# Two norms of a two-layer decoder trunk: sums with tokens on the partitions, the root on four columns, the result spread by products

## The chip, the cores and the metric

The kernel runs on one core of one Trainium2 chip, as one launch for the whole model of two layers. The metric is the device time of that launch in microseconds (us). TensorE (PE) multiplies, VectorE (DVE) and ScalarE (ACT) read its accumulation banks and work on SBUF, and GpSimd (POOL) does almost nothing after the start. SyncE (SP) issues the loads of weights.

## The reference, cut to what matters

x has 512 tokens of 1024 channels. Each of the two layers computes three token mixers in parallel, a cross-attention on 256 memory tokens and a SwiGLU feed-forward part. Two of its norms are touched here:

```
def gmlp(uv_in, ln_g, ln_b, w_s, b_s):
    u, v = split(gelu(uv_in), 2)
    mu  = mean(v, axis=-1)
    var = mean((v - mu)**2, axis=-1)
    v   = (v - mu) * rsqrt(var + EPS) * ln_g + ln_b        # 512 channels
    ...                                                    # mixing within chunks of 128 tokens
    return u * mixed

def mla(c_q, ...):
    q = (rms_norm(c_q, q_norm) @ w_uq)                     # c_q has 384 channels
    ...
rms_norm(x, g) = x * rsqrt(mean(x*x) + EPS) * g
```

So for every token a sum over channels is needed, then root and reciprocal, then that number is applied to every channel of the token.

## The kernel before, in words

All activations lie transposed: channels on the 128 partitions, the 512 tokens along the free axis, so a tile is 128 x 512 in fp32. A weight matrix is cut in units of 128 output columns. For a unit SP loads `raw` (three slots), ScalarE rounds it to `wH` (`split`, L964), VectorE makes the rest `wL` (`weight_low`, L1370), and TensorE makes three products for each 128 input channels, `wH` with `hH`, `wH` with `hL`, `wL` with `hH` (L577 to L579), with 512 columns each. A unit with 1024 input channels has 24 products.

`PLAN` is a list of steps that every engine walks. TensorE walks it as it stands. VectorE and ScalarE walk `READERS_PLAN`, the same list with four norm steps moved a little ahead. Each engine does for a step only what is its own, strictly in order, with a wait on a counter wherever it needs another engine's result. TensorE's results go to seven banks in rotation (`take`): each taking waits for the reader of the bank's previous content. `LEFT_OUT` and `known["pad"]` keep the slots and the rotation the same for both passes of the layer loop.

A sum over channels is a sum over partitions. The usual way in this kernel: VectorE and ScalarE add up the squares of the tiles into one tile of 128 x 512, TensorE multiplies it by a 128 x 128 matrix of ones, `ones`, as one fp32 product of 512 columns, so that every partition of the bank holds the sum of every token. ScalarE takes the root of the 128 x 512 bank into a tile, and VectorE its reciprocal.

**The gated unit (gMLP).** `v` is `gv`, four tiles, `u` is `gu`, four tiles. `gm_mean` (L697) is the sum for the mean. VectorE subtracts it (L1470), ScalarE squares (L1106), VectorE adds into `gsum` (L1475). `gm_var`, after the unit `gu` 2, is the product of ones (L697), the root on ScalarE into `rstd` (L1110), the reciprocal on VectorE (L1479), four products of `gv` with `rstd` (L1482) and four scalings (L1485). `gm_vt` later transposes `gv` on TensorE (L703), ScalarE copies it to `gvt` (L1114), and `gm_mix` (L711) mixes the tokens. Between them stand the forget gate of the recurrent mixer (`f_2` on ScalarE: L1092 to L1098; `f_3` on VectorE: `hk`, `hlf`, L1513, L1518), pieces of the rotary angles (`angle`, VectorE L1346 to L1363), the units `gu` 3, `hi`, `hq` and `hg`, and `sin`, in which VectorE makes `segM` (L1457) that the first `hg_exp` product reads (L738).

**The queries' norm.** `norm_q`, after the unit `ckv` 0, is the product of ones with `sqs` (L799), the root into `rstd` (L1182), the reciprocal (L1594). The evictions of the query heads (`mq`, L1333) multiply by `rstd`.

**The key-value norm** is done in the other way already. `norm_kv` (L805) makes four products in which the 128 tokens of a block of `ytmp` are the stationary side and one column of `ones` streams, so that tokens land on partitions and the bank has four columns. Root (L1185) and reciprocal (L1597) work on 128 x 4. `rkv` (L811) spreads a column along the tokens by four products of the column, broadcast to 128 x 128, with the identity `ident`, and ScalarE copies the bank to the tile `rkv` (L1190).

`mst` is four columns of the tile `columns`. An fp32 product appears in the trace as two records.

Of the kernel before, what the change touches and what calls it, by code (L numbers as in the profile page):

```python
# [24 lines left out]
ACT = mybir.ActivationFunctionType  # L25
AX = mybir.AxisListType

P = 128
DM, T, L, NM = 1024, 512, 2, 256
EPS = 1e-6  # L30
KT = DM // P
TT = T // P
QR, KVR, NOPE, ROPE, VD, HA = 384, 256, 64, 32, 64, 8
HG, CH = 4, 64
# [70 lines left out]
def plan():  # L105

    u = lambda name, j=0: ("u", name, j)
    p = [("lb",), u("gv", 0), u("gv", 1), ("norm", "mix"), u("gv", 2), u("gv", 3), ("angle", 0), u("hf", 0), ("gm_sum",), ("gm_ws",)]
    p += [u("gu", 0), ("gm_mean",), u("gu", 1), ("f_1", 0), u("gu", 2), ("gm_var",), ("f_2", 0), ("angle", 1), u("gu", 3), ("f_3", 0), ("angle", 2)]
# [12 lines left out]
    p += [("cq_split",), u("ckv", 0), ("norm_q",), u("ckv", 1), u("kr"), ("kr_swap",), u("q", 0), ("norm_kv",), ("hg_norm", HG - 1)]  # L122
# [81 lines left out]
def build(nc, a, out, known):  # L204
# [7 lines left out]
    with ExitStack() as ctx:  # L212
# [10 lines left out]
        def did(engine, *step):  # L223

            count[engine] = count.get(engine, 0) + 1
            counted["mark"][step] = (engine, phase[0], count[engine])
            return sem(engine + "_done"), 1

        def after(l, *step):

            engine, of, n = mark.get(step, ("tensor", "before", 1))
            s = sem(engine + "_done")
            if of == "before":
                return s, n
            b, t = base.get(engine, 1), total.get(engine, 1)
            if of == "after":
                return s, b + L * t + n
            if phase[0] == "after":
                return s, b + (L - 1) * t + n
            return s, l * t + (b + n)  # L240
# [168 lines left out]
        def bank(*step):  # L409
            return PS[:, bank_of.get(step, 0), :]  # L410
# [106 lines left out]
        def _(pe):  # L517
# [4 lines left out]
            def take(l, step, reader, keep=False):  # L522


                b = 7 if keep else turn[0] % 7
                turn[0] += not keep
                if fresh[b]:

                    pe.wait_ge(*before(l, *last_reader.get(b, ("x0", 0))))
                elif readers[b]:  # L530
                    pe.wait_ge(*after(l, *readers[b]))
                fresh[b] = False
                readers[b] = reader
                counted["bank"][step] = b
                return PS[:, b, :]
# [135 lines left out]
            with pe.Fori(0, L) as l:  # L671
# [3 lines left out]
                for step in PLAN:  # L675
# [18 lines left out]
                    elif kind in ("gm_mean", "gm_var"):  # L694
                        o = take(l, (kind,), ("gm_c", 3) if kind == "gm_mean" else ("gm_std",))
                        pe.wait_ge(*after(l, kind + "_sum"))
                        nc.tensor.matmul(o, ones[:], gsum[:], start=True, stop=True).then_inc(*did("tensor", kind))  # L697
                    elif kind == "gm_vt":
# [97 lines left out]
                    elif kind == "norm_q":  # L796
                        o = take(l, (kind,), (kind + "_std",))
                        pe.wait_ge(*after(l, kind + "_sum"))
                        nc.tensor.matmul(o, ones[:], sqs[:], start=True, stop=True).then_inc(*did("tensor", kind))  # L799
# [125 lines left out]
        def _(act):  # L925
# [51 lines left out]
            with act.Fori(0, L) as l:  # L977
# [16 lines left out]
                for step in READERS_PLAN:  # L994
# [113 lines left out]
                    elif kind == "gm_var":  # L1108
                        act.wait_ge(*after(l, "gm_var"))
                        nc.scalar.activation(rstd[:], bank("gm_var"), ACT.Sqrt, scale=1.0 / 512, bias=EPS).then_inc(*did("scalar", "gm_std"))  # L1110
# [68 lines left out]
                    elif kind == "norm_q":  # L1179
                        act.wait_ge(*after(l, kind))  # L1180
                        act.wait_ge(*after(l, "o_n", HG - 2))
                        nc.scalar.activation(rstd[:], bank(kind), ACT.Sqrt, scale=1.0 / QR, bias=EPS).then_inc(*did("scalar", kind + "_std"))  # L1182
# [101 lines left out]
        def _(dve):  # L1284
# [87 lines left out]
            with dve.Fori(0, L) as l:  # L1372
# [12 lines left out]
                for step in READERS_PLAN:  # L1385
# [91 lines left out]
                    elif kind == "gm_var":  # L1477
                        dve.wait_ge(*after(l, "gm_std"))
                        V.reciprocal(rstd[:], rstd[:]).then_inc(*did("vector", "gm_rstd"))  # L1479
                        dve.wait_ge(*own(l, "vector"))  # L1480
# [111 lines left out]
                    elif kind == "norm_q":  # L1592
                        dve.wait_ge(*after(l, "norm_q_std"))
                        V.reciprocal(rstd[:], rstd[:]).then_inc(*did("vector", "norm_q_r"))  # L1594
# [84 lines left out]
                    elif kind == "u":  # L1679
# [51 lines left out]
                        elif name == "q":  # L1731
                            dve.wait_ge(*after(l, *step))
                            dve.wait_ge(*own(l, "vector"))
# [91 lines left out]
```

## Time and profile before

| | |
|---|---|
| median of 3 runs | 2244.11 us (2242.25 to 2244.37) |
| the profiled execution, its own time | 2240.72 us |
| its span, first to last instruction | 2238.9 us |
| granted TensorE clock, mean | 0.995 |
| busy: PE, DVE, ACT, POOL | 2195.5 us, 1341.1 us, 995.3 us, 9.2 us |
| HBM traffic over the span | 87 GB/s |

The page tells for each engine how long it was busy, and follows the chain of work that ended last back from the end. The timeline lists instructions of one engine in order of time, with the start, the duration, and in brackets the idle time of the engine before it and what ended it. Neighbouring instructions of the same kind are merged with a count (x4). PEld is the loading of TensorE's stationary side, which overlaps the products.

### The profile page before, as it was taken

How to read it: one execution, taken by the hardware profiler on the slowest of the kernel's cores; microseconds unless marked ns; L12 is line 12 of the kernel's file. 1: busy time of each engine (PE TensorE's matmuls, PEld its weight loads, DVE VectorE, ACT ScalarE, POOL GpSimd, SP SyncE). 2: the span in 40 equal slices, each digit the busy share in tenths (PEclk: the TensorE clock that was granted, in tenths of full speed). 3: DMA queues.
4: the chain of work that ended last, by engine and by line, in shares of the span. 5: the costliest groups of instructions: out<-in, count | busy, mean ns of one | idle time of the engine just before them, and what ended most of it. 6: DMA issues, size and time to landing. Idle time of an engine off the chain costs nothing.

```text
span 2238.9 us, 31689 instructions
## 1 busy us (share of the span) xinstructions
PE 2195.5 (98%) x10441; PEld 1785.5 (80%) x10441; DVE 1341.1 (60%) x2099; ACT 995.3 (44%) x1451; POOL 9.2 (0%) x12
## 2 busy tenths in 40 slices
PE   7999999999999999999999999999999999999998
PEld 6877787778888888888877877777788888888887
DVE  7867777666565544443378677776666655444432
ACT  5665545454443433322255555454444443233223
POOL 1000000000000000000000000000000000000000
PEclk9999999999999999999999999999999999999999
DMA  6222222224343233333252222122343333333331
GB/s 177 64 76 57 67 59 58 61 73 120 106 122 95 83 111 99 95 90 102 83 136 59 67 66 71 43 56 68 101 116 100 114 94 94 95 103 95 97 95 64
DMA packets 368238, 197.55 MB, mean 88 GB/s; under 512 B 24284, under 2 KB 361544, under 8 KB 368072
## 3 DMA queue, kind: packets, MB, share of 16 engines
q1 hardware_dynamic: 362584, 185.81, 29.8%
q10 hardware_dynamic: 5488, 9.64, 1.4%
q8 instruction: 90, 1.47, 0.3%
q14 instruction: 76, 0.62, 0.1%
HBM read 192.14 MB, written 2.10 MB: 87 GB/s over the span
## 4 chain that ended last, share of the span: by engine, by line
PE 85%; DVE 7%; issue 4%; ACT 3%; DMA 0%; DVEq 0%; ACTq 0%; SPq 0%
PE PS L577 24%; PE PS L579 24%; PE PS L578 24%; PE PS L823 2%; PE PS L846 2%; PE PS L758 1%; DVE attn L1556 1%; DVE rstd L1576 1%; DVE mprod L1552 1%; DVE dec L1538 1%; PE PS L833 1%; PE PS L652 1%; PE PS L654 1%; PE PS L653 1%; ACT wH L964 1%
## 5 line engine op out<-in xcount | busy, mean ns | idle before, releaser
L964 ACT ACTIVATE wH<-raw 128x1024 fp32r<-128x1024 f32 (+4 forms) x406 | 384.1, 947 | 943.9 <-PE PS L579 908.6
L577 PE MATMUL PS<-hH,wH 128*128 128x512 f32 (+1 forms) x1680 | 666.8, 397 | 4.8 <-DVE gate L1333 3.4
L579 PE MATMUL PS<-hH,wL 128*128 128x512 f32 (+1 forms) x1680 | 656.0, 390 | 0.0
L578 PE MATMUL PS<-hL,wH 128*128 128x512 f32 (+1 forms) x1680 | 655.7, 390 | 0.0
L1370 DVE TENSOR_TENSOR wL<-raw,wH 128x1024 fp32r<-128x1024 f32 (+4 forms) x406 | 437.4, 1078 | 177.8 <-ACT wH L964 177.1
L577 PEld LDWEIGHTS PS<-hH,wH 128*128 128x128 f32 (+1 forms) x1680 | 316.1, 188 | 76.6 <-DVE gate L1333 4.3
L578 PEld LDWEIGHTS PS<-hL,wH 128*128 128x128 f32 (+1 forms) x1680 | 316.2, 188 | 67.1 <-issue 2.9
L579 PEld LDWEIGHTS PS<-hH,wL 128*128 128x128 f32 (+1 forms) x1680 | 315.8, 188 | 67.4
L1333 DVE TENSOR_TENSOR gate<-PS,rh 128x512 f32<-128x512 f32 x92 | 63.6, 691 | 154.6 <-PE PS L579 154.0
L579 PE MATMUL PS<-fH,wL 128*128 128x512 f32 x352 | 136.9, 389 | 0.0
L577 PE MATMUL PS<-fH,wH 128*128 128x512 f32 x352 | 136.9, 389 | 0.0
L578 PE MATMUL PS<-fL,wH 128*128 128x512 f32 x352 | 136.9, 389 | 0.0
L1316 DVE TENSOR_TENSOR xT<-xT,PS 128x512 f32<-128x512 f32 x48 | 33.0, 688 | 132.4 <-PE PS L579 132.4
L1333 DVE TENSOR_TENSOR fm<-PS,rh 128x512 f32<-128x512 f32 x44 | 30.4, 691 | 131.2 <-PE PS L579 131.2
L578 PEld LDWEIGHTS PS<-fL,wH 128*128 128x128 f32 x352 | 66.1, 188 | 13.8
L577 PEld LDWEIGHTS PS<-fH,wH 128*128 128x128 f32 x352 | 66.1, 188 | 13.7
L579 PEld LDWEIGHTS PS<-fH,wL 128*128 128x128 f32 x352 | 66.1, 188 | 13.6
L1556 DVE TENSOR_REDUCE attn<-mprod 128x128 f32<-128x896 f32 x32 | 56.2, 1756 | 1.1
L577 PE MATMUL PS<-mgH,wH 128*128 128x512 f32 x128 | 49.8, 389 | 0.0
L578 PE MATMUL PS<-mgL,wH 128*128 128x512 f32 x128 | 49.8, 389 | 0.0
L579 PE MATMUL PS<-mgH,wL 128*128 128x512 f32 x128 | 49.8, 389 | 0.0
L577 PE MATMUL PS<-xoH,wH 128*128 128x512 f32 x128 | 49.8, 389 | 0.0
(354 smaller groups left out, 3256.0 us busy)
## 6 DMA issues: line engine op xcount, KB each, us to landing
raw<-in_w_in SPq DMA_DIRECT2D x106, 512.0 KB, 3.9
raw<-in_ffn_w_in SPq DMA_DIRECT2D x88, 512.0 KB, 3.8
raw<-in_xa_w_kv SPq DMA_DIRECT2D x32, 512.0 KB, 3.8
raw<-in_ffn_w_out SPq DMA_DIRECT2D x32, 512.0 KB, 3.9
raw<-in_w_mix_out SPq DMA_DIRECT2D x16, 512.0 KB, 4.1
raw<-in_xa_w_q SPq DMA_DIRECT2D x16, 512.0 KB, 4.2
raw<-in_xa_w_o SPq DMA_DIRECT2D x16, 512.0 KB, 3.9
raw<-in_ffn_w_out SPq DMA_DIRECT2D x16, 384.0 KB, 3.3
```

The source lines that it names most:

```text
L577: nc.tensor.matmul(o, w0, xh(k0 + k), start=(first and k == 0), stop=False)
L578: nc.tensor.matmul(o, w0, xl(k0 + k), start=False, stop=False)
L579: ins = nc.tensor.matmul(o, w1, xh(k0 + k), start=False, stop=(last and k == kts - 1))
L652: nc.tensor.matmul(xv_banks[i], xh, w0, start=(kk_ == 0), stop=False)
L653: nc.tensor.matmul(xv_banks[i], xh, w1, start=False, stop=False)
L823: nc.tensor.matmul(o[:, 0:n], mq[0:96, h % 2, i * P:n], mk[0:96, h % 2, 0:n], start=True, stop=False)
L846: ins = nc.tensor.matmul(oa_bank[r, kb * P:T], mv[:, kb, h * VD:(h + 1) * VD], mpt[:, PT_OFF[kb]:PT_OFF[kb] + n], start=(kb == 0), stop=(k ...
L964: nc.scalar.activation(wH[:, PLACE[n] % NS, 0:w], raw[:, PLACE[n] % NR, 0:w], ACT.Copy).then_inc(*did("scalar", "hi", n))
L1316: V.tensor_tensor(xT[:, j, :], xT[:, j, :], bank(*step) if name != "fo" else bank("fo", j), ALU.add)\
L1333: V.tensor_tensor(dst, src, scale, ALU.mult).then_inc(*did("vector", *me))
L1370: V.tensor_tensor(wL[:, s, 0:w], raw[:, r, 0:w], wH[:, s, 0:w].bitcast(F32), ALU.subtract).then_inc(sem("weights_low"), 1)
L1556: V.tensor_reduce(attn[:, i, :], mprod[:].rearrange("p n t -> p t n"), AX.X, ALU.add)\
```

## The change

The variance of the gated unit and the queries' norm are computed as the key-value norm is. Four products with one streaming column each take the place of the product with `ones`. Root and reciprocal work on `mst`, 128 x 4. Two new steps spread the result: `gm_rs`, after the unit `gu` 3, and `rq`, after the unit `ckv` 1. In each, TensorE makes four products of a broadcast column with `ident`, and ScalarE copies the bank to `rstd`. The eight operations of VectorE on `gv` move from the step `gm_var` to `gm_rs`. The eviction of the first query head waits for `rq`.

```diff
-    p += [u("gu", 0), ("gm_mean",), u("gu", 1), ("f_1", 0), u("gu", 2), ("gm_var",), ("f_2", 0), ("angle", 1), u("gu", 3), ("f_3", 0), ("angle", 2)]
+    p += [u("gu", 0), ("gm_mean",), u("gu", 1), ("f_1", 0), u("gu", 2), ("gm_var",), ("f_2", 0), ("angle", 1), u("gu", 3), ("gm_rs",), ("f_3", 0), ("angle", 2)]
...
-    p += [("cq_split",), u("ckv", 0), ("norm_q",), u("ckv", 1), u("kr"), ("kr_swap",), u("q", 0), ("norm_kv",), ("hg_norm", HG - 1)]
+    p += [("cq_split",), u("ckv", 0), ("norm_q",), u("ckv", 1), ("rq",), u("kr"), ("kr_swap",), u("q", 0), ("norm_kv",), ("hg_norm", HG - 1)]
...
+                    elif kind == "gm_var":
+                        o = take(l, (kind,), ("gm_std",))
+                        pe.wait_ge(*after(l, kind + "_sum"))
+                        for i in range(TT):
+                            ins = nc.tensor.matmul(o[:, i:i + 1], gsum[:, i * P:(i + 1) * P], ones[:, 0:1], start=True, stop=True)
+                        ins.then_inc(*did("tensor", kind))
+                    elif kind in ("gm_rs", "rq"):
+                        o = take(l, (kind,), (kind,))
+                        pe.wait_ge(*after(l, "gm_rstd" if kind == "gm_rs" else "norm_q_r"))
+                        for i in range(TT):
+                            ins = nc.tensor.matmul(o[:, i * P:(i + 1) * P], mst[:, i:i + 1].broadcast_to([P, P]), ident[:], start=True, stop=True)
+                        ins.then_inc(*did("tensor", kind + "_b"))
...
-                        nc.tensor.matmul(o, ones[:], sqs[:], start=True, stop=True).then_inc(*did("tensor", kind))
+                        for i in range(TT):
+                            ins = nc.tensor.matmul(o[:, i:i + 1], sqs[:, i * P:(i + 1) * P], ones[:, 0:1], start=True, stop=True)
+                        ins.then_inc(*did("tensor", kind))
...
-                        nc.scalar.activation(rstd[:], bank("gm_var"), ACT.Sqrt, scale=1.0 / 512, bias=EPS).then_inc(*did("scalar", "gm_std"))
+                        nc.scalar.activation(mst, bank("gm_var")[:, 0:TT], ACT.Sqrt, scale=1.0 / 512, bias=EPS).then_inc(*did("scalar", "gm_std"))
+                    elif kind in ("gm_rs", "rq"):
+                        act.wait_ge(*after(l, kind + "_b"))
+                        if kind == "rq":
+                            act.wait_ge(*after(l, "o_n", HG - 2))
+                        nc.scalar.activation(rstd[:], bank(kind), ACT.Copy).then_inc(*did("scalar", kind))
...
-                        act.wait_ge(*after(l, "o_n", HG - 2))
-                        nc.scalar.activation(rstd[:], bank(kind), ACT.Sqrt, scale=1.0 / QR, bias=EPS).then_inc(*did("scalar", kind + "_std"))
+                        nc.scalar.activation(mst, bank(kind)[:, 0:TT], ACT.Sqrt, scale=1.0 / QR, bias=EPS).then_inc(*did("scalar", kind + "_std"))
...
-                        V.reciprocal(rstd[:], rstd[:]).then_inc(*did("vector", "gm_rstd"))
-                        dve.wait_ge(*own(l, "vector"))
+                        V.reciprocal(mst, mst).then_inc(*did("vector", "gm_rstd"))
+                    elif kind == "gm_rs":
+                        dve.wait_ge(*after(l, "gm_rs"))
...
-                        V.reciprocal(rstd[:], rstd[:]).then_inc(*did("vector", "norm_q_r"))
+                        V.reciprocal(mst, mst).then_inc(*did("vector", "norm_q_r"))
...
+                            if j == 0:
+                                dve.wait_ge(*after(l, "rq"))
```

**VectorE in the gated unit**, the order of its instructions before, from the low part of a weight at the end of `gu` 2 on (`turns` belongs to the angles; a REGISTER_ALU row sets up a wait; line numbers are each kernel's own):

```order
L1370 TENSOR_TENSOR wL<-raw,wH 128x1024
L1478 REGISTER_ALU
L1479 RECIPROCAL rstd<-rstd 128x512
L1480 REGISTER_ALU
L1482 TENSOR_TENSOR gv<-gv,rstd 128x512 x4
L1483 REGISTER_ALU
L1485 TENSOR_SCALAR gv<-gv,cur 128x512 x4
L1452 REGISTER_ALU
L1357 TENSOR_SCALAR turns<-turns 32x512
```

and with the change, from the last angle operations of that step on:

```order
L1470 REGISTER_ALU
L1377 SCALAR_TENSOR_TENSOR red_148<-turns,red_148 32x512
L1470 REGISTER_ALU
L1377 SCALAR_TENSOR_TENSOR red_148<-turns,red_148 32x512
L1702 REGISTER_ALU
L1351 TENSOR_TENSOR gu<-PS,rh 128x512
L1387 REGISTER_ALU
L1388 TENSOR_TENSOR wL<-raw,wH 128x1024
L1499 REGISTER_ALU
L1501 TENSOR_TENSOR gv<-gv,rstd 128x512 x4
L1502 REGISTER_ALU
L1504 TENSOR_SCALAR gv<-gv,cur 128x512 x4
```

The eight operations on `gv` stood before the angle step and the eviction of `gu` 3. They now stand behind both and behind the low part of the next weight, with a wait of their own ahead of them (L1499).

**ScalarE in the same place**, before, from the high part of a weight at the start of `gu` 3 on:

```order
L957 REGISTER_ALU
L961 REGISTER_ALU
L964 ACTIVATE wH<-raw 128x1024
L1004 REGISTER_ALU
L1006 ACT_TABLE_LOAD
L1006 ACTIVATE gu<-gu 128x512
L957 REGISTER_ALU
L961 REGISTER_ALU
L964 ACTIVATE wH<-raw 128x1024
```

and with the change:

```order
L971 REGISTER_ALU
L975 REGISTER_ALU
L978 ACTIVATE wH<-raw 128x1024
L1018 REGISTER_ALU
L1020 ACT_TABLE_LOAD
L1020 ACTIVATE gu<-gu 128x512
L1126 REGISTER_ALU
L1129 ACTIVATE rstd<-PS 128x512
L971 REGISTER_ALU
L975 REGISTER_ALU
L978 ACTIVATE wH<-raw 128x1024
```

The copy of the spread root (L1129) stands right behind the activation of `gu` 3 and ahead of the next weight.

## Rows read from the trace of the kernel before

**Rows 1.** The page: busy time of the engines, and the chain by engine.
```profile
PE 2195.5 (98%) x10441; PEld 1785.5 (80%) x10441; DVE 1341.1 (60%) x2099; ACT 995.3 (44%) x1451; POOL 9.2 (0%) x12
...
PE 85%; DVE 7%; issue 4%; ACT 3%; DMA 0%; DVEq 0%; ACTq 0%; SPq 0%
```

**Rows 2.** TensorE's waits: who for whom, us in total, times, longest.
```profile
PE PS L738 <- DVE segM L1457: 2.1, 2, 1.0
```

**Rows 3.** Timeline, TensorE at `gm_var`: start us, us, engine, line, operation [idle before].
```profile
68.62 0.39 PE L579 MATMUL PS<-hH,wL 128*128 128x512 f32 x1
68.85 1.02 PE L697 MATMUL PS<-gsum,ones 128*128 128x512 f32 x2
...
69.94 0.40 PE L578 MATMUL PS<-hL,wH 128*128 128x512 f32 x1
```

**Rows 4.** Timeline, TensorE at `norm_kv` and the head norm behind it.
```profile
348.39 0.40 PE L579 MATMUL PS<-cqH,wL 128*96 128x512 f32 x1
348.63 0.95 PE L805 MATMUL PS<-ones,ytmp 128*128 128x1 f32 x8
349.44 1.10 PE L795 MATMUL PS<-onrm,ones 128*128 128x512 f32 x2
...
350.62 0.39 PE L578 MATMUL PS<-ckL,wH 128*64 128x512 f32 x1
```

**Rows 5.** Timeline, TensorE at `rkv`.
```profile
351.30 0.40 PE L578 MATMUL PS<-ckL,wH 128*64 128x512 f32 x1
351.53 0.40 PE L579 MATMUL PS<-ckH,wL 128*64 128x512 f32 x1
351.77 1.05 PE L811 MATMUL PS<-ident,columns 128*128 128x128 f32 x8
...
352.89 0.39 PE L632 MATMUL PS<-wL,ckH 128*128 128x512 f32 x1
```

**Rows 6.** The tile `columns`: duration ns min/median/max, first and last start.
```profile
L1185 ACT ACTIVATE columns<-PS x2: 173/174/174, 349.6 to 1452.7; 128x4 f32<-128x4 f32 x2
L1597 DVE RECIPROCAL columns<-columns x2: 165/166/166, 350.0 to 1453.0; 128x4 f32<-128x4 f32 x2
```

**Rows 7.** Timeline, VectorE at the unit `kr`, after the queries' norm.
```profile
346.83 0.69 DVE L1333 TENSOR_TENSOR krt<-PS,rh 96x512 f32<-96x512 f32 x1 [0.50 <-PE PS L579]
```

**Rows 8.** Timeline, VectorE from `gm_var` to `segM`, first layer.
```profile
72.57 3.35 DVE L1479 RECIPROCAL rstd<-rstd 128x512 f32<-128x512 f32 x1 [1.21 <-ACT rstd L1110]
75.96 2.50 DVE L1482 TENSOR_TENSOR gv<-gv,rstd 128x512 f32<-128x512 f32 x4
...
80.44 0.42 DVE L1357 TENSOR_SCALAR turns<-turns 32x512 f32<-32x512 f32 x1
...
84.78 0.48 DVE L1513 TENSOR_SCALAR hk<-hk,lbc 128x512 f32<-128x512 f32 x1
...
96.50 1.23 DVE L1370 TENSOR_TENSOR wL<-raw,wH 128x1024 fp32r<-128x1024 f32 x1 [1.36 <-ACT wH L964]
...
98.24 0.68 DVE L1457 CAST segM<-seg 128x1024 fp32r<-128x1024 f32 x1
```

**Rows 9.** Timeline, ScalarE from `gm_var` to `hq`, first layer.
```profile
71.94 0.60 ACT L1110 ACTIVATE rstd<-PS 128x512 f32<-128x512 f32 x1
...
78.67 1.28 ACT L1006 ACT_TABLE_LOAD   x1
83.77 0.63 ACT L1006 ACTIVATE gu<-gu 128x512 f32<-128x512 f32 x1 [3.81 <-DVE gu L1333]
84.31 1.05 ACT L964 ACTIVATE wH<-raw 128x1024 fp32r<-128x1024 f32 x1
...
92.94 0.63 ACT L1010 ACTIVATE hq<-hq 128x512 f32<-128x512 f32 x1 [4.73 <-DVE hq L1333]
```

**Rows 10.** Timeline, TensorE at the transposes of `gv` and at `segM`.
```profile
86.08 1.91 PE L703 MATMUL PS<-ident,gv 128*128 128x128 f32 x16
...
99.05 0.49 PE L738 MATMUL PS<-segM,lfH 128*128 128x512 f32 x1 [1.04 <-DVE segM L1457]
```

More of the change, by code:

```diff
@@ L693, in _ @@
                         ins.then_inc(*did("tensor", "gm_ws"))
-                    elif kind in ("gm_mean", "gm_var"):
-                        o = take(l, (kind,), ("gm_c", 3) if kind == "gm_mean" else ("gm_std",))
+                    elif kind == "gm_mean":
+                        o = take(l, (kind,), ("gm_c", 3))
                         pe.wait_ge(*after(l, kind + "_sum"))
                         nc.tensor.matmul(o, ones[:], gsum[:], start=True, stop=True).then_inc(*did("tensor", kind))
+                    elif kind == "gm_var":
[10 more added lines that the diff above has]
+                        ins.then_inc(*did("tensor", kind + "_b"))
                     elif kind == "gm_vt":
```

## The prediction

> **What bounds the kernel now.** I read the page's busy shares and its chain first [rows 1]: TensorE is busy for 98% of the span and carries 85% of the chain that ended last, VectorE 7%, ScalarE 3%. So a microsecond added to TensorE's own stream counts in full, and a microsecond taken from VectorE counts only where TensorE waits for VectorE. I then asked for TensorE's waits. In the two stretches that the change touches one wait stands: the product on `segM` waits for VectorE, 2.1 us in the two layers together [rows 2]. After the queries' norm no wait of TensorE hangs on it. Last I read the timelines of both stretches, engine by engine, to price the operations and to follow VectorE's queue to that wait. In the gated unit's stretch VectorE is far behind TensorE: ScalarE waits 3.81 us for the eviction of the last `gu` and starts on it at 83.77 [rows 9], while TensorE, with 22 steps of 0.23 us after 69.94 [rows 3], was through with it by 75.4.
>
> **TensorE, what goes.** At each place one fp32 product of 512 columns is removed. [rows 3] show it between two ordinary products: L579 starts at 68.62, the next L578 at 69.94. An ordinary step is 0.23 us (351.30 to 351.53 in [rows 5]), and two would have taken 0.46, so the product costs 1.32 - 0.46 = 0.86 us.
>
> **TensorE, what comes.** The kernel already does both new kinds of product for the key-value norm. Sums by columns: in [rows 4] L579 starts at 348.39 and the second ordinary product after the group at 350.62, 2.23 us later. Off go 0.46 for two steps and 0.86 for the 512-column product L795 in between: 0.91 us for four sums (eight records). The spread: in [rows 5] L579 starts at 351.53 and L632 at 352.89, 1.36 us; less 0.46 it is 0.90 us for four products of 128 columns. Both are priced by the very same forms in the same kind of neighbourhood, so I take these values. The bounds are nothing at all, if they hid beside their neighbours, and the whole 0.95 and 1.05 us that the two groups span in [rows 4, 5], if nothing overlapped: 0.19 more or 1.81 less a place than these values. **Net 0.91 + 0.90 - 0.86 = 0.95 us a place**, four places (two in each of two layers): 3.8 us of TensorE time, if every one of them reaches the end.
>
> The Trainium skill's page "TensorE: Matmul & The Clock Gate" (Back-to-back issue gap) gives a warm product of 1 to 64 columns some 25 ns and one of 128 columns 56 ns, start to start, when it is isolated from weight loads. By that, eight and eight records would make 0.65 us where the trace has 1.81, and the net would be -0.21 us a place. The trace disagrees, since here each of these products brings its own weights [rows 4, 5]; I go by the rows.
>
> **VectorE and ScalarE at the queries' norm.** The 3.35 us reciprocal becomes one on four columns, 0.17 us [rows 6], the root 0.17 instead of 0.60, and a copy of 0.60 comes in. It is worth nothing: a few VectorE operations later VectorE sits idle 0.50 us until TensorE has finished `krt` [rows 7], so it had already caught up, and from there on everything follows TensorE. The first reader of the spread norm, the eviction of `q` head 0, comes only after `krt` in VectorE's order, and ScalarE's copy stands two units ahead of it. So both layers pay the full 0.95: **+1.9 us**.
>
> **VectorE and ScalarE in the gated unit.** Here the order matters. Before, VectorE runs [rows 8]: reciprocal at 72.57, four products with `rstd` from 75.96, four scalings up to 80.44, angle, last `gu` eviction, low part of a weight, then `hk` at 84.78. From the reciprocal to `hq` the timeline gives it no idle time, and the wait of [rows 2] is the end of that queue: `hq` late, so ScalarE's `Silu` waits 4.73 us for it [rows 9], behind it the four `gvt` copies and a weight's high part, then VectorE's low part (idle 1.36 for it), `lfL`, `segM` at 98.24, and TensorE starts at 99.05 after 1.04 us of idleness [rows 8, 10].
>
> The change takes 3.35 - 0.17 + 0.43 = 3.6 us off VectorE's start of this queue. But it moves the eight operations on `gv` behind the last `gu` step, and makes them wait for ScalarE's copy of the spread root, which stands behind ScalarE's exponentials, one weight, the table load for `Gelu` and `Gelu` itself. That queue has no wait in it: it only shifts by the shorter root. The load of [rows 9] at 78.67 comes at 78.67 - 0.43 = 78.24 and lasts 1.28; `Gelu` starts at 79.52 (its `gu`, which TensorE finishes at 75.4, is evicted well before), the copy at 80.06 (0.54 later, as the weight follows `Gelu` in [rows 9]), and it ends 0.60 later at 80.66. VectorE starts the products with `rstd` at 80.69 and needs 80.44 - 75.96 = 4.48 us for the eight: `hk` starts at 85.17 instead of 84.78. **VectorE's queue is 0.39 us later, not 3.6 earlier**: it now idles first for the weight's high part, then for the copy. Behind the waiting products on VectorE are `hk`, `hlf`, the angle and `hq`; all of them move by 0.39, and `segM` with them. TensorE arrives 0.95 later, at 98.96 instead of 98.01, and starts at 99.05 + 0.39 = 99.44. So of its 0.95 only 0.39 remains, the rest goes into the stall, which shrinks from 1.04 to 0.5 us. The transposes of `gv`, 86.08 before and 87.03 now [rows 10], find the whole of `gv` finished at 85.2, with 1.9 us to spare. Two layers: **+0.8 us**. ScalarE's extra copy needs no table load of its own, since a weight is copied right behind `Gelu`, at 84.31, without one [rows 9].
>
> Other edits cost nothing: each layer takes two more accumulation banks, in rotation, but every bank that comes up earlier was read out long before (the nearest readers belong to the unit before last or earlier), and the padding that squares the rotation at the layer's end falls among the output units, where TensorE waits for nothing. No DMA is added.
>
> **Sum.** 1.9 + 0.8 = +2.7 us. Against the profiled execution, 2240.72 us, that is 2243.4; the median of the three runs is 2244.11, so I say **2246.8 us**. About 0.2%, 4.5 us, is what a measurement of this kernel can tell from no change, so this is within it.
>
> **Rivals.**
> 1. VectorE's relief does arrive (the copy is earlier than I reckon, or the queue is not tied to it). For: 3.6 us are really taken off. Then TensorE finds `segM` ready but for 1.04 - 0.95 = 0.09 us, and each layer gains 0.09 there: 1.9 - 0.2 = +1.7, 2245.8 us. Against: ScalarE's queue of [rows 9] has no slack to give.
> 2. Slower by over 0.2%: the hand-over through ScalarE is the new bound. If the copy of the spread root costs one more table load (1.28, as each in [rows 9]), or waits that long for anything, VectorE's queue and `segM` are 0.39 + 1.28 = 1.67 us late in each layer, and TensorE with them: 1.9 + 3.3 = +5.2, 2249.3 us. It decides from 1.3 us of lateness a layer (4.5 = 1.9 + 2 x 1.3), a copy 0.9 us later than reckoned. For: the copy is the last in a row of seven operations and two table loads, and VectorE is strictly in order. Against: [rows 9], and the compiled order has no load between `Gelu` and the copy.
> 3. The small products hide beside their neighbours and cost next to nothing. Then the queries' norm gains 0.86 in each layer, the gated unit stays on VectorE's 0.39: -1.7 + 0.8 = -0.9, 2243.2 us. [rows 4, 5] speak against it. This is the side to which the page named above leans.
> 4. The change doesn't do what it says, in time: TensorE pays 0.95 everywhere and VectorE's queue plays no part, because the stall is not the queue's end. +3.8, 2247.9 us.
>
> **Chances.** The forecast, with rival 4 as its near neighbour, 0.70; rival 1 0.12; rival 3 0.03; rival 2 0.11; the rest, mostly a measurement that is off by more than the runs show, 0.04. All but rival 2 and part of the rest lie within 4.5 us: same 0.84, slower 0.12, faster 0.04. Even the lower bounds of every part together, -0.86 twice and -0.09 twice, give -1.9 us, so faster needs a disturbance. The range goes from 2243.0 (rival 3) to 2250.0 (rival 2 and 0.7 for the scatter of the runs).
>
> **What would show it.** In the profile after: each sum group and each spread group at some 0.9 us of TensorE; VectorE idle before the products of `gv` with `rstd`, ended by ScalarE's copy; `hk` 0.4 us later than before; the wait on `segM` down to about 0.5 us a layer, all in both layers; `krt` still waiting for TensorE. Wrong would be: the wait on `segM` grown or gone, a wait of TensorE before the transposes of `gv`, a table load beside the new copy, or a span that moves by more than 4.5 us.

## The result

| | kernel before | changed kernel |
|---|---|---|
| median, fastest and slowest of 20 runs each on one chip | 2242.15 us (2238.51 to 2245.55) | 2246.11 us (2243.35 to 2249.52) |
| span of the profiled execution | 2238.9 us | 2242.8 us |
| granted TensorE clock, mean | 0.995 | 0.995 |

The ratio is 1.0018, 95% interval 1.0011 to 1.0025: 4.0 us slower (2.5 to 5.6). The prediction was +2.7 us and 2246.8 us. The kernel before ran here 2 us below the median shown ahead of the prediction, so it is the difference that is to be compared, not the closeness of the two totals. The changed kernel's 20 runs had a mean granted clock of 0.9940; for the 20 runs of the kernel before beside them the clock is not on record, and in 62 later runs it was 0.9946. So up to about 1 us of the 4.0 may be clock.

The page of the changed kernel answers to [rows 1]:

```profile
PE 2199.1 (98%) x10497; PEld 1791.5 (80%) x10497; DVE 1328.9 (59%) x2099; ACT 996.3 (44%) x1455; POOL 9.1 (0%) x12
...
PE 80%; DVE 9%; issue 5%; ACT 4%; DMA 1%; ACTq 0%; DVEq 0%; SPq 0%
```

VectorE has 12.2 us less to do, TensorE 3.6 us more, close to the 3.9 us by which the span grew. The chain is now followed further along VectorE, but that is one way back among several that end together; it says nothing of where the 4 us come from. The waits of TensorE (who for whom, us in total, times, longest) say more:

```profile
PE PS L750 <- DVE segM L1475: 1.2, 2, 0.8
...
PE PS L837 <- DVE mq L1631: 0.6, 1, 0.6
```

The wait of [rows 2] went from 2.1 to 1.2 us (0.45 in the first layer, 0.80 in the second), and there is one that the kernel before does not have: the first scores of the latent attention wait for VectorE's rotated queries, `mq`.

TensorE at `gm_var` and at the first spread, first layer (start us, us, engine, line, operation):

```profile
68.42 0.39 PE L579 MATMUL PS<-hH,wL 128*128 128x512 f32 x1
68.65 0.95 PE L702 MATMUL PS<-ones,gsum 128*128 128x1 f32 x8
...
69.78 0.40 PE L578 MATMUL PS<-hL,wH 128*128 128x512 f32 x1
...
74.81 0.39 PE L579 MATMUL PS<-hH,wL 128*128 128x512 f32 x1
75.04 1.05 PE L708 MATMUL PS<-ident,columns 128*128 128x128 f32 x8
...
76.17 0.39 PE L578 MATMUL PS<-hL,wH 128*128 128x512 f32 x1
```

These answer to [rows 3 to 5]. The sums take 69.78 - 68.42 - 0.46 = 0.90 us, the spread 76.17 - 74.81 - 0.46 = 0.90 us. Predicted were 0.91 and 0.90.

VectorE from the reciprocal on, beside [rows 8], with the idle time before an operation and what ended it in brackets:

```profile
71.94 0.18 DVE L1497 RECIPROCAL columns<-columns 128x4 f32<-128x4 f32 x1 [0.78 <-ACT columns L1124]
...
78.06 1.23 DVE L1388 TENSOR_TENSOR wL<-raw,wH 128x1024 fp32r<-128x1024 f32 x1 [2.13 <-ACT wH L978]
80.49 2.50 DVE L1501 TENSOR_TENSOR gv<-gv,rstd 128x512 f32<-128x512 f32 x4 [1.20 <-ACT rstd L1129]
...
84.86 0.48 DVE L1532 TENSOR_SCALAR hk<-hk,lbc 128x512 f32<-128x512 f32 x1
...
98.33 0.68 DVE L1475 CAST segM<-seg 128x1024 fp32r<-128x1024 f32 x1
```

And ScalarE ahead of them, beside [rows 9]:

```profile
78.04 1.28 ACT L1020 ACT_TABLE_LOAD   x1
79.34 0.63 ACT L1020 ACTIVATE gu<-gu 128x512 f32<-128x512 f32 x1
79.88 0.58 ACT L1129 ACTIVATE rstd<-PS 128x512 f32<-128x512 f32 x1
```

VectorE saved 3.2 us on the reciprocal and stood idle for 2.13 + 1.20 of them, first for a weight's high part and then for the copy of the spread root. `hk` starts at 84.86, where it was 84.78. No table load came with the copy. TensorE at `segM`, beside [rows 10]:

```profile
94.96 3.74 PE L723 MATMUL PS<-gwT,gvt 128*128 128x128 f32 x32
99.14 0.49 PE L750 MATMUL PS<-segM,lfH 128*128 128x512 f32 x1 [0.45 <-DVE segM L1475]
...
1203.03 0.49 PE L750 MATMUL PS<-segM,lfH 128*128 128x512 f32 x1 [0.80 <-DVE segM L1475]
```

The second layer is not a copy of the first. There ScalarE's table load ahead of the root starts 1.76 us later than before (1174.34 against 1172.58) while TensorE is 1.43 us later, so 0.33 us of lateness was in the queue before the change acted, and it comes out at `segM`: 0.80 instead of 0.45.

**Where the 3.9 us of the span lie.** The unit products can be paired one by one between the two kernels. The start of one, changed kernel less kernel before, is a curve that moves only where something differs. It starts at -0.24 us (-0.20 ahead of the gated unit's sums) and ends at +3.82:

| place | shift of TensorE | 1st layer | 2nd layer |
|---|---|---|---|
| gated unit, from the sums to the spread group | up | +0.98 | +0.97 |
| wait for `segM` smaller | down | -0.69 | -0.35 |
| queries' norm | up | +0.91 | +0.91 |
| first scores, `mq` late | up | 0 | +0.50 |
| between the layers, a DMA issue of ScalarE (below) | up | +0.45 | |
| half clock at other places (below) | both | | -1.26 + 1.60 |

The rest, +-0.1 us at a time, is drift. The first three lines, the ones that the prediction priced, make +2.7 us; the other three make +1.3.

### The profile page after: what moved, and what is told of

It reads as the page before. It is cut to its first block, busy times and chain, and to the rows that moved or that the text cites. A ratio compares the mean times of both kernels' runs of the same rounds, so it can differ in the third digit from the quotient of the medians.

```text
span 2242.8 us, 31821 instructions
## 1 busy us (share of the span) xinstructions
PE 2199.1 (98%) x10497; PEld 1791.5 (80%) x10497; DVE 1328.9 (59%) x2099; ACT 996.3 (44%) x1455; POOL 9.1 (0%) x12
## 4 chain that ended last, share of the span: by engine, by line
PE 80%; DVE 9%; issue 5%; ACT 4%; DMA 1%; ACTq 0%; DVEq 0%; SPq 0%
PE PS L577 23%; PE PS L578 23%; PE PS L579 23%; PE PS L860 2%; PE PS L837 2%; PE PS L770 1%; DVE attn L1575 1%; DVE mprod L1571 1%; DVE rstd L1595 1%; DVE dec L1557 1%; PE PS L847 1%; ACT wH L978 1%; PE PS L654 1%; PE PS L652 1%; PE PS L653 1%
## 5 line engine op out<-in xcount | busy, mean ns | idle before, releaser
L579 PE MATMUL PS<-hH,wL 128*128 128x512 f32 (+1 forms) x1680 | 655.2, 390 | 0.0
L579 PEld LDWEIGHTS PS<-hH,wL 128*128 128x128 f32 (+1 forms) x1680 | 315.5, 188 | 67.1
L579 PE MATMUL PS<-fH,wL 128*128 128x512 f32 x352 | 136.9, 389 | 0.0
L579 PEld LDWEIGHTS PS<-fH,wL 128*128 128x128 f32 x352 | 66.1, 188 | 13.7
L579 PE MATMUL PS<-mgH,wL 128*128 128x512 f32 x128 | 49.8, 389 | 0.0
```

What stands on the lines that cost most here:

```text
L579: ins = nc.tensor.matmul(o, w1, xh(k0 + k), start=False, stop=(last and k == kts - 1))
```

## The experiments

Ten further runs were made: nine other kernels, and the changed one once more. Differences of 1 us are at the edge of what such runs tell, so each verdict rests on the ratio with its interval and on the shift curve of the trace. A third number, called "at equal clock" below, comes from a line put through the 161 runs whose clock is on record, without those of the last two kernels (time against the run's mean granted clock, one level for each kernel; for the kernel before these are the 62 runs of the later rounds): 1.83 us less for each 0.001 of clock, with a scatter of 0.96 us that is left. By it the changed kernel is 3.0 us (+-0.5) slower than the one before. It is an adjustment worked out after the runs, not a measurement of its own, and it is fair only if a kernel doesn't itself change how often the clock falls, which was not tried.

### Each half alone

`e1_gated_only` keeps the gated unit's half of the change and puts the queries' norm back, `e2_queries_only` the reverse.

```
 e1   norm_q:  matmul(o, ones[:], sqs[:]) ; Sqrt -> rstd ; reciprocal(rstd)        # as before
      PLAN:    ... u("ckv", 1), u("kr") ...                                        # no ("rq",)
 e2   gm_var:  matmul(o, ones[:], gsum[:]) ; Sqrt -> rstd ; reciprocal(rstd), gv * rstd
      PLAN:    ... u("gu", 3), ("f_3", 0) ...                                      # no ("gm_rs",)
```

> The gated unit's part of the change alone; the queries' norm is as before. Theory (TensorE's own price, less what the wait on segM swallows): each layer pays 0.9 us of TensorE, and the wait on segM shrinks from 1.04 to about 0.5 us, so 0.3 to 0.4 us a layer remain, +0.6 to +0.8 us against the kernel before. Rival (TensorE pays everything): +1.9 us, and the wait on segM stays at 1.04. In the trace: TensorE is +0.9 later behind the spread in the first layer and +0.3 to +0.4 later from segM on, against the kernel before, and krt and the first scores show no further step.

> The queries' norm alone in the new way; the gated unit is as before. Theory: 0.95 us of TensorE in each layer, all of it in the end, +1.9 us against the kernel before; VectorE's 3.2 us a layer are worth nothing. Rival (VectorE's relief is worth something behind it, at the rotary chain and the first scores): between 0 and +1. In the trace: one step of +0.9 to +1.0 us of TensorE in each layer, between the units ckv 0 and kr, and no step in the gated unit.

Measured: `e1_gated_only` 1.0002 of the time before (0.9993 to 1.0011), at equal clock +0.6 us (+-0.6); `e2_queries_only` 1.0004 (0.9995 to 1.0014), at equal clock +1.8 us (+-0.6). Neither half can be told from no change by the ratio alone. The traces are sharper. In the gated half the shift goes from -0.88 to +0.11 at the spread and to -0.59 at `segM`: +0.29 net, with the wait at 0.44 and 0.46 us in the two layers. In the queries' half it goes from -0.49 to +0.43 and stays, +0.92 and +0.91 in the two layers, and `segM` keeps its 1.04 us. Two halves make 0.6 + 1.8 = 2.4, the whole 3.0: additive within the errors. Neither half's trace has a wait for `mq` at the first scores, so 0.5 us of what is left may be that wait.

### The changed kernel once more

> The changed kernel once more, for a second profile of the same program. The theory is that only two steps of the first comparison belong to the change: one spread group a place, +0.90 us each, less what comes back at segM. Those steps must stand again: TensorE idle 0.45 before the first product with segM in both layers, and the spread groups at 0.90. The rival is that everything between the two profiles belongs to the change: the 1.1 us by which ScalarE's DMA issue of seg was longer at the layer boundary, the 0.5 us at the first scores, and the two stretches at half clock (1233.4 to 1236.5 and 1318.7 to 1321.9). By the first theory these three stand elsewhere or are gone in this profile; by the rival they stand at the same places with the same sizes.

One run, 2244.03 us, span 2242.3. The places of the change stand at +0.91 to +0.97 us, the wait for `segM` at 0.47 and 0.60. Of the other steps, **one does not repeat and two do**. The layer boundary costs nothing here, with ScalarE's issue of `seg` at 1.38 us (it was 1.99 in the first profile, and 0.52 to 1.95 in kernels with nothing of the change). The two stretches at half clock stand where they were and as long: the granted clock is 0.88 from 1226 to 1240 us and 0.88 from 1311 to 1325 in both profiles. They are not the change's for all that: `e4_segm_early` and `e9_angle_alone`, which hold nothing of it, have 0.88 and 0.88 too, and it is the profile of the kernel before that differs, with 0.76 and 1.00. (Another stretch, at 213 us in the first profile, stands at 130 us in this one.) And the late `mq` is here again, in both layers:

```profile
PE PS L837 <- DVE mq L1631: 1.4, 2, 0.8
```

So the theory was wrong on the first scores, which belong to the change after all, and the rival on the boundary; the repeated half clock, which the rival had right, comes from something that the kernels have in common.

### The wait at the first scores

Before the scores two DMAs on ScalarE's queue swap the halves of the queries. ScalarE's queue in the changed kernel, first and second layer:

```profile
359.12 1.16 ACTq L1192 DMA_DIRECT2D spare<-mq  x2
...
1464.54 1.67 ACTq L1192 DMA_DIRECT2D spare<-mq  x2
```

The second issue is 0.5 us longer; the key-value norm's copy, `mk` and the rotation stand behind it, and TensorE waits. Instructions themselves come by DMA, on a queue of their own (page of the changed kernel):

```profile
q8 instruction: 90, 1.47, 0.3%
```

Ninety packets, one in 25 us. Their moment, read in half microseconds, against the issue:

| kernel, layer | packet on q8 | issue, its length | from TensorE's last L579 before the scores to the next L579 |
|---|---|---|---|
| before, both | none near | 358.15 and 1461.22, 1.16 | 3.58 and 3.61 |
| changed, 1st | 360.0 to 360.5 | 359.12, 1.16 | 3.59 |
| changed, 2nd | 1464.5 to 1465.0 | 1464.54, **1.67** | 4.12 |
| changed again, 1st | 359.0 to 359.5 | 358.66, **1.64** | 4.09 |
| changed again, 2nd | 1464.0 to 1464.5 | 1463.73, **1.88** | 4.33 |
| queries alone, 2nd | 1469 | 1461.15, 1.16 | |

(None near: none from 345 us to the first layer's scores, and none within 10 us of the second issue.) Four rows are few, but there are eight such pairs of issues in a layer, and with 12 traces 192 of them. In 180 no packet of q8 was under way during the pair, and it took 1.15 to 1.17 us every time. In the other 12 one was: ten of these took longer, 1.21 to 2.33 us, and the two that did not had their packet start in the last 0.3 us. The kernel before has one too (2.30 us at 369.64, and TensorE doesn't wait there). A kernel with products added ahead should move the packet off the issue. That is one of the two last kernels, and both also double a suspected cost:

```
 e10  norm_q:       for i in range(TT)   ->  for i in list(range(TT)) * 2      # the four sums twice
 e11  gm_rs, rq:    for i in range(TT)   ->  for i in list(range(TT)) * 2      # the four spreads twice
```

> The changed kernel with the four one-column sums of the queries' norm issued twice (same result). Two things are read. First the price of such a group in TensorE's stream: 0.90 us more at the queries' norm of each layer than the changed kernel shows there (+0.95 against the kernel before, so +1.85 in this one). Second the wait of TensorE for mq at the first scores. Theory: it is there because a transfer of instructions (queue q8, one every 25 us or so) lies at the same moment as ScalarE's DMA issue for the swap of the queries' halves, at 359 to 361 and at 1464 us in the changed kernel, and at 366 us or later in the queries' part alone; the issue then takes 1.6 to 1.9 us instead of 1.16. Four more products before it bring that transfer some 4 us earlier, away from the issue: the issue is back at 1.16 us, TensorE's wait for mq is gone in the first layer, and the whole is +0.9 x 2 - 0.5 to -1.2. Rival: the longer issue comes with the kernel's two new steps together, by whatever cause but not by that transfer's place, and stands here again at 1.6 us or more with the wait of 0.6 to 0.8 us.

Measured: the shift against the changed kernel rises from 3.70 to 4.59 (first layer) and from 7.41 to 8.30 (second) at the norm, 0.89 us for one more group. The sums twice, on TensorE's timeline:

```profile
338.16 0.39 PE L579 MATMUL PS<-hH,wL 128*128 128x512 f32 x1
338.39 1.84 PE L812 MATMUL PS<-ones,sqs 128*128 128x1 f32 x16
...
340.42 0.40 PE L578 MATMUL PS<-hL,wH 128*128 128x512 f32 x1
```

340.42 - 338.16 - 0.46 = 1.80 us for two groups. And the other half of the question:

```profile
363.71 1.16 ACTq L1192 DMA_DIRECT2D spare<-mq  x2
...
1472.84 1.16 ACTq L1192 DMA_DIRECT2D spare<-mq  x2
```

The packets start at 362.35 and 1471.40 us, ahead of the issues, moved by 2.3 and 1.8 us against them and not by the 4 expected; both issues are short, the wait for `mq` is gone, and the stretch at the scores takes 3.60 and 3.59 us again. In the changed kernel's first profile the first layer was short already, so this takes the wait away where it had been in three layers of four. The total is not to be read (one run, 2252.57 us at a clock of 0.992: some 3 us each were lost at half clock at 277 and at 1387 us, where the changed kernel's profile has no such stretch).

> The changed kernel with the four spread products issued twice in both places, in the gated unit and in the queries' norm. Theory: each doubled group costs TensorE 0.90 us once more at its place. In the gated unit the copy of the root is that much later for ScalarE and VectorE, but the values stood ready there with under 1 us to spare, so the wait at segM grows or stays: +0.9 at the spread, and of that 0.4 or less comes back at segM. At the queries' norm +0.9 more stays to the end. In all +2.5 to +3.6 us against the changed kernel. The transfer of instructions on q8 lies 8 products, some 8 us, earlier than in the changed kernel, and the issue for the queries' swap is at 1.16 us. Rival: the second group hides behind the weight loads of the first and adds less than half of 0.90.

One run, 2245.04 us, span 2243.3: **only +0.5 us on the span** of the changed kernel, where +2.5 to +3.6 had been expected. The price of a doubled group was right, +0.89 to +0.91 at each of the four places. What was wrong was the part given back. At `segM` all of it came back, 0.91 us in the first layer and 1.04 in the second, at the layer boundary 0.42, and at the second layer's scores another 0.51, since the packets start at 357.15 and 1462.64 us, ahead of the issues at 359.93 and 1465.54 (3.7 and 3.3 us earlier against them, where 8 had been expected), and both issues take 1.16. TensorE's timeline before `segM`'s product:

```profile
95.80 3.74 PE L723 MATMUL PS<-gwT,gvt 128*128 128x128 f32 x32
99.29 0.47 PE L750 MATMUL PS<-segM,lfH 128*128 128x512 f32 x1
```

So at the wait for `segM` the changed kernel still had 0.9 us to give, although its row says 0.45. The queue of VectorE did not move (`hk` at 84.82 us against 84.86), as the prediction's reading has it: the copy of the root waits for `Gelu` on ScalarE, not for TensorE.

### What a row of idle time is worth

`e3_rs_ahead` is the changed kernel in which ScalarE copies the spread root ahead of its work on `gu` 3, and VectorE multiplies by it ahead of its own. `e4_segm_early` is the kernel before, with the cast of `segM` in step `gm_ws`, long before it is needed.

```
 e3   READERS_PLAN: (("norm", "ffn"), 2), (("rkv",), 1), + (("gm_rs",), 1)
 e4   step "sin":   - V.tensor_copy(segM[:], seg[:])
      step "gm_ws": + V.tensor_copy(segM[:], seg[:])
```

> The changed kernel with one edit: ScalarE and VectorE take the step gm_rs ahead of gu 3 (one entry in the list of moved steps). Theory (VectorE's queue is set by ScalarE's copy, which stands behind a weight, a table load and Gelu): the copy comes at about 77.0 instead of 79.9 us, the products with rstd at 77.6 instead of 80.5, hk 1.1 us earlier (the eviction of gu 3 and a weight's low part now stand ahead of it), the wait on segM disappears in both layers, and TensorE gains what is left of it, 0.45 and up to 0.8 us: -0.9 to -1.2 us against the changed kernel, so +1.5 to +3 against the kernel before. Rival (the wait on segM has another cause): the copy comes earlier and the wait stays.

> The kernel before, with one edit: VectorE makes segM in the step gm_ws, 44 us earlier, instead of at the end of its queue. Theory (the wait on segM is the end of VectorE's queue): TensorE then waits for lfL, 0.6 us earlier, so -0.6 us a layer, -1.2 us in all against the kernel before. Rival (the wait belongs to segM itself, its load or its making): the wait goes entirely, -1.0 us a layer, -2.1 us.

Measured: `e3_rs_ahead` 1.0004 of the time before (0.9995 to 1.0013), at equal clock 2.6 us below the changed kernel; more than expected. `e4_segm_early` 0.9989 (0.9980 to 0.9998). Their timelines at `segM` explain the first:

```profile
94.82 3.74 PE L723 MATMUL PS<-gwT,gvt 128*128 128x128 f32 x32
98.31 0.47 PE L750 MATMUL PS<-segM,lfH 128*128 128x512 f32 x1
```

That is `e3_rs_ahead`. First below is the mix in the kernel before, whose product on `segM` is at 99.05 [rows 10], then `e4_segm_early`, where the wait is now for VectorE's `lfL`:

```profile
94.20 3.81 PE L711 MATMUL PS<-gwT,gvt 128*128 128x128 f32 x32
...
93.82 3.81 PE L711 MATMUL PS<-gwT,gvt 128*128 128x128 f32 x32
98.16 0.49 PE L738 MATMUL PS<-segM,lfH 128*128 128x512 f32 x1 [0.53 <-DVE lfL L1338]
```

From the first product of the mix to the first with `segM`, first layer:

| kernel | idle in the row | from mix to `segM` | more than without a wait |
|---|---|---|---|
| before | 1.04 | 4.85 us | 1.36 |
| with the early cast | 0.53 | 4.34 | 0.85 |
| changed | 0.45 | 4.18 | 0.69 |
| `e3_rs_ahead`, and the doubled spread | none | 3.49 | 0 |

**A stop cost some 0.3 us more here than its idle row says** (0.24 to 0.32): the row of idle time begins when the last product is through, while in the unbroken stream of `e3_rs_ahead` the product on `segM` starts at 98.31, 0.25 us before the row of the mix ends (94.82 + 3.74). The ends of such rows are modelled, so the distances between starts are what counts. Behind the eight products on `segM` the kernel before loses another 0.26 us: 0.39 and 0.33 us to the next two unit products instead of 0.23 each in `e3_rs_ahead`. In all it lost 1.6 us a layer here, not 1.04. The expectations below reckon with 1.5.

With that known, three versions were made to take the loss away.

```
 e7   the gated unit's half of the change + e3's entry + e4's early cast
 e8   the kernel before + e4's early cast + READERS_PLAN: (("angle", 1), 2)
 e9   the kernel before                    + READERS_PLAN: (("angle", 1), 2)
```

The entry for `angle` lets VectorE do the angles' second step (2.5 us) ahead of the reciprocal, in the 1.21 us in which it waits for ScalarE's root [rows 8].

> The gated unit's part of the change alone (the queries' norm as in the kernel before), with VectorE's multiplies by the spread root taken ahead of its reading of gu 3, and segM made from seg back in step gm_ws. A stop of TensorE has cost more in the runs so far than its idle row says: from the first product of the mix to the first product with segM TensorE took 4.85 us with a row of 1.04, 4.18 with 0.45 and 3.49 with none, so a row of 1.04 hides a loss of 1.36, and another 0.15 lies behind the products with segM. Theory: this kernel pays +0.90 a layer for the spread group and gets the whole 1.5 back, so -0.6 a layer, -1.2 us in all, 0.9995 of the time before, with no idle row before segM's product and the span from mix to segM at 3.49. Rival: the early cast of segM takes 0.7 us of VectorE at a place where something else waits, and the gain is half or none: 1.0000.

> The kernel before, nothing of the change in it: segM made from seg back in step gm_ws, and VectorE takes the angles' second step (four operations, 2.5 us) ahead of the reciprocal for the gated unit, into the 1.2 us that it stood idle there. Theory: the stall before segM's products was VectorE's queue and nothing else, and both edits together remove 0.7 and 1.2 us of that queue, more than the 1.36 us that the stall cost; TensorE goes from the mix to the products with segM in 3.49 us instead of 4.85 and starts behind them without the gap of 0.15, -1.5 us a layer, -3.0 us in all, 0.9987 of the time before. Rival: the angles' step is longer than the idle time it fills, the reciprocal and with it the multiplies for the gated unit's values come 1.3 us later, and TensorE waits for them at the transposes (1.3 us a layer) instead: 1.0000 to 1.0012.

> The kernel before with the angles' second step alone taken ahead of the reciprocal by VectorE; segM is made where it was. Theory: VectorE reaches segM 1.2 us earlier, the idle row of 1.04 before segM's product shrinks to 0 to 0.2 us, and the kernel gains 0.9 to 1.2 us a layer, some -2.1 us, 0.9991. Rival as for both together: the reciprocal is late for the transposes and TensorE waits there, 1.0000 to 1.0012.

| kernel | ratio to before, 95% | shift at `segM`, layer 1, layer 2 | at equal clock |
|---|---|---|---|
| `e7_gated_ahead_segm` | 0.9988 (0.9978 to 0.9997) | -0.71, -0.72 | -3.3 (+-0.6) |
| `e8_seg_and_angle` | 0.9985 (0.9976 to 0.9994) | -1.68, -1.70 | -4.5 (+-0.6) |
| `e9_angle_alone` | 0.9996 (0.9987 to 1.0005) | -1.28, -1.30 | -3.2 (+-0.6) |

In `e8_seg_and_angle` the loss is gone, with nothing of the change in it. TensorE:

```profile
93.89 3.74 PE L711 MATMUL PS<-gwT,gvt 128*128 128x128 f32 x32
97.38 0.47 PE L738 MATMUL PS<-segM,lfH 128*128 128x512 f32 x1
```

VectorE, whose idle time of 1.21 before the reciprocal is filled:

```profile
71.12 0.42 DVE L1357 TENSOR_SCALAR turns<-turns 32x512 f32<-32x512 f32 x1
71.58 0.68 DVE L1359 SCALAR_TENSOR_TENSOR red<-turns,ang 32x512 f32<-32x512 f32 x1
72.29 1.40 DVE L1359 SCALAR_TENSOR_TENSOR red<-turns,red 32x512 f32<-32x512 f32 x2
73.73 3.35 DVE L1477 RECIPROCAL rstd<-rstd 128x512 f32<-128x512 f32 x1
```

Its median is 2239.81 us against 2241.93 for the kernel before, and its ratio 0.0015 below one: two steps of VectorE put in another order, with no arithmetic saved, are faster than both kernels by the ratio, and as fast as any version tried. The rival, a late `gv` at the transposes, did not come. In `e9_angle_alone` the row of idle time is gone, but the 0.26 us behind the products on `segM` stays, so those do not belong to the row.

All three kernels, and `e4_segm_early` (-2.0 +-0.6 against -1.2 on its curve), gain more at equal clock than their curves show at `segM`, by 0.6 to 1.9 us. Two things make this excess. One is a second wait, before the next head's product on `segM`, for VectorE's `mprod`: 0.69 us in the kernel before, 0.20 in `e7_gated_ahead_segm` in the second layer and none in the first, 0.48 in `e8_seg_and_angle`, 0.67 in `e9_angle_alone`. The curve gives it 1.2 us in `e7`, 0.2 us in each layer of `e8`, nothing in `e9`.

```profile
1223.54 0.50 PE L750 MATMUL PS<-segM,lfH 128*128 128x512 f32 x1 [0.20 <-DVE mprod L1568]
```

The other is the adjustment. The mean times of `e7`, `e8`, `e9` and `e4_segm_early` lie 2.4, 3.1, 1.4 and 1.8 us below the kernel before (62 runs), which leaves `e8` and `e9` no excess at all, and the adjustment adds 0.9, 1.4, 1.8 and 0.3, because these kernels' runs had a lower mean clock (0.9941, 0.9938, 0.9936, 0.9945 against 0.9946). Whether the kernels themselves lower it was not tried, so their gains are known to 1 or 2 us and no better.

## Why the prediction was right or wrong

The verdict (no change beyond 0.2%) was right by a narrow margin: 0.18%, and the interval of the ratio reaches to 0.25%. The differences, +2.7 forecast, +4.0 (2.5 to 5.6) measured and +3.0 (+-0.5) at equal clock, agree within the errors. In the trace the places that the forecast priced make +2.7 us, but in part by luck: in the gated unit the first layer kept less than forecast and the second more. Point by point:

- **Prices of the groups: right.** 0.91 and 0.90 forecast, 0.90 and 0.90 found, 0.89 to 0.91 for each of the six groups added in the last two kernels. The Trainium skill's page "TensorE: Matmul & The Clock Gate" (Back-to-back issue gap) gives 25 ns for a product of up to 64 columns when it is isolated from weight loads; by that, an estimate, the eight one-column records would cost 0.2 us. Doubled they cost 0.9 us more, 0.11 us a record. The same section says that the isolated gap is too small where each product has a weight load, and gives about 81 ns at 128 columns there. That was the figure to compare, and the 0.11 us of the rows is above it too. Rival 3 is out.
- **Queries' norm: right.** VectorE's 3.2 us bought nothing, `krt` waits for TensorE as before (by 2.33 us now, not 0.50), and TensorE pays +0.91 in both layers against 0.95.
- **Gated unit, VectorE's queue: the mechanism right, the size a little off.** Forecast was 0.39 later; against TensorE's own start (0.20 us earlier in this profile) it is some 0.3 in the first layer: the copy took 0.58 us instead of 0.60. In the second layer it is 0.6, since ScalarE came to the root 0.33 us late. TensorE kept 0.29 and 0.62 us where 0.39 each had been forecast. Rival 1 (the relief arrives) needed the queue free of ScalarE's copy. `e3_rs_ahead` comes closest to that, with the copy at 76.86 instead of 79.88 and VectorE's multiplies moved with it, and TensorE got 1.7 us back at `segM` in each layer: the place of this step in the two engines' order kept the relief away.
- **"The stall shrinks from 1.04 to 0.5": right by the row in the first layer (0.45), not in the second (0.80), and the step behind it was wrong.** I took a stall for what its row says. That mattered little for the forecast, since both kernels stall and the excess of 0.3 us cancels. It decided a later estimate: the doubled spread was expected to cost 0.5 to 0.9 us a layer in the gated unit and cost nothing.
- **"Other edits cost nothing ... no DMA is added": wrong.** The added products moved TensorE's stream of instructions, and with it a packet of q8, onto ScalarE's issue for the queries' swap. It cost 0.5 to 0.7 us in three of the changed kernel's four layers profiled, 0.5 us in the first profile and 1.2 in the second. This term stood neither in the sum nor among the rivals. What it makes of the median of 20 runs is not known, as only two were profiled.
- **Rival 2 (over 0.2% slower)** did not happen by its mechanism, the compiled order had no load and the trace shows none. **Rival 4** (TensorE pays everywhere, +3.8) has the nearest number to the raw +4.0 and is refuted by the curve: 0.69 and 0.35 us did come back at `segM`, and 0.9 and 1.0 more in the doubled kernel. By the profile, what lies above the forecast's +2.7 is the late `mq` (0.5), the layer boundary (0.45, which did not repeat) and half clock (0.3).

## What to carry to other kernels

When one engine is busy 98% of the span, price an edit by its added time on that engine, and ask of each relief elsewhere which queue carries it to a wait; here a 3.4 us reciprocal vanished and nothing moved, because the next step waited for another engine's copy. A better lever was the order in which the waited-for engine works: filling its idle time and taking one cast out of the last steps gained 1.7 us a layer. Judge a stall by the distance between the products around it and compare with a kernel where it is gone, not by its idle row.

## What the runs showed of the hardware

- **Scatter and clock.** Runs of one kernel spread over 7 us, and this goes with the mean granted clock: of the changed kernel's 20 runs the eight at 0.995 average 2244.5 us, the eight at 0.993 average 2247.7. In the trace this is a few short stretches at half clock. In the kernel before, the recurrent mixer of the second layer makes TensorE wait 1.71 us for `gate`, and then:

```profile
1231.89 0.63 PE L578 MATMUL PS<-hL,wH 128*128 128x512 f32 x1
1232.32 0.63 PE L579 MATMUL PS<-hH,wL 128*128 128x512 f32 x1
```

  The products are 0.43 us apart instead of 0.23, for 6 us on end (granted 0.50 from 1231 to 1237 us, 0.97 in the 6 us behind), the lower level, 1.2 GHz. In the changed kernel it is half as long there, and another such stretch stands at 1319 to 1322 us; both stand again in its second profile, and in those of kernels with nothing of the change, while a third moved from 213 to 130 us. So places are partly the same from run to run and partly not. By the curves one costs 1.2 to 3.2 us, which is the size of the effect in question. It is why a comparison of this kernel to 0.1% needs ten runs or more and the clock beside them.
- **The fetch of instructions meets a DMA issue.** Of 192 pairs of issues on ScalarE's queue, the 180 with no packet of q8 under way took 1.15 to 1.17 us, and ten of the 12 with one took 1.21 to 2.33. The packet's place goes with the products in TensorE's program. Against the start of the first layer's issues it starts 12.2 us behind in the kernel before, 9.4 with the gated half, 7.9 with the queries' half, 0.4 to 0.9 with both (also in `e3_rs_ahead`, where both layers' pairs take 1.90), 1.4 ahead with the sums doubled, 2.8 ahead with the spreads doubled. In the last two the wait is gone in all four layers. What the two contend for was not tried, nor whether another effect of the added products did it.
